# Sums of squares taken inside the embedding stage, two norm stages joined into their neighbours, and block 2's first layer opened on halves of the tokens

## The reference, cut to what matters

```python
for i in range(DEPTH):                      # block 1, DEPTH = 2
    h = rms_norm(x, g_mix[i])
    ... mixer, experts ...
    ple_gate = sigmoid(rms_norm(x, g_ple[i]) @ w_ple_gate[i])
    x = x + ple_gate * (p[i] @ w_ple[i])    # embedding stage
x = rms_norm(x, g_final)
...
for l in range(DEPTH):                      # block 2
    u = rms_norm_2(x, norm_g[l]) * (1 + scale) + shift
    z = u @ w_in[l]
    ... x = x + gate * (merged @ w_out[l])
```

## Time and profile before

| | us |
|---|---|
| median of three runs | 3681.98 (3681.97 to 3682.17) |
| profiled execution, its own time | 3682.63 |
| span of its profile | 3680.9 |
| VectorE's last addition in layer 0's embedding stage, start | 1143.27 |
| layer 1's first product, start | 1164.03 |
| the same addition in layer 1's embedding stage, start | 2278.16 |
| block 2's first product, start | 2310.16 |

### The profile page before, as it was taken

One profiled execution on the slowest core, in us unless ns is written; L12 is line 12 of the kernel. 1 busy time (PEld: TensorE's weight loads), 2 busy tenths in 40 slices (PEclk: granted clock), 3 DMA queues, 4 the chain that ended last, 5 costly groups with the idle time before them and its releaser, 6 DMA issues. The chain is left out here.

```text
span 3680.9 us, 41926 instructions
## 1 busy us (share of the span) xinstructions
PE 3421.2 (93%) x16364; PEld 2281.5 (62%) x16364; DVE 1760.2 (48%) x3023; ACT 1064.4 (29%) x1684; POOL 38.6 (1%) x42
## 2 busy tenths in 40 slices
PE   7999996999988999996999997999999999999999
PEld 5866673444446866675444445777766687777666
DVE  7766633212135875744121224467654355666443
ACT  4343322101023334322011013343333234433322
POOL 1000000000000200000000000000000000000000
PEclk9999998999998999997999998999999999999999
DMA  5521127999963441124999982212321331222213
GB/s 191 193 94 58 58 86 310 423 423 424 424 250 129 157 144 58 58 94 189 420 424 424 423 351 71 93 61 66 92 81 69 106 115 58 68 76 86 69 69 115
DMA packets 129376, 653.28 MB, mean 177 GB/s; under 512 B 22036, under 2 KB 32276, under 8 KB 62136
## 3 DMA queue, kind: packets, MB, share of 16 engines
q1 hardware_dynamic: 129208, 650.98, 45.6%
HBM read 632.54 MB, written 14.72 MB: 176 GB/s over the span
## 5 line engine op out<-in xcount | busy, mean ns | idle before, releaser
L1733 PE MATMUL ps<-normed_T_hi,ring_split 128*128 128x512 f32 x1920 | 609.8, 399 | 7.5 <-PEq L264 7.5
L1733 PEld LDWEIGHTS ps<-normed_T_hi,ring_split 128*128 128x128 f32 x1920 | 354.5, 188 | 107.4 <-issue 34.3
L1733 PE MATMUL ps<-normed_T_lo,ring_split 128*128 128x512 f32 (+1 forms) x960 | 376.1, 392 | 0.0
L2486 PE MATMUL ps<-normed_T_hi,ring_split 128*128 128x512 f32 x1024 | 336.1, 410 | 8.9 <-DVE branches L2752 7.6
L2065 DVE TENSOR_TENSOR ring_split<-weight_ring,ring_split 128x2048 fp32r<-128x2048 f32 x76 | 174.0, 2289 | 151.9 <-ACT ring_split L1921 151.6
L2486 PEld LDWEIGHTS ps<-normed_T_hi,ring_split 128*128 128x128 f32 x1024 | 192.9, 192 | 81.6 <-issue 32.7
L1733 PEld LDWEIGHTS ps<-normed_T_lo,ring_split 128*128 128x128 f32 (+1 forms) x960 | 180.2, 188 | 40.0
L2486 PE MATMUL ps<-normed_T_lo,ring_split 128*128 128x512 f32 x512 | 202.6, 396 | 0.0
L1789 PE MATMUL ps<-branches 128*128 128x512 f32 x384 | 173.0, 593 | 3.3 <-issue 3.0
L1230 PE MATMUL ps<-weight_ring,projected 128*64 128x512 f32 x768 | 167.9, 593 | 0.0
L1921 ACT ACTIVATE ring_split<-weight_ring 128x2048 fp32r<-128x2048 f32 x76 | 144.9, 1912 | 52.5 <-DMA weight_ring<-in_w_slabs 48.1
(11 more groups left out here) (443 smaller groups left out, 6028.3 us busy)
## 6 DMA issues: line engine op xcount, KB each, us to landing
weight_ring<-in_w_slabs SPq DMA_DIRECT2D x78, 1024.0 KB, 4.9
weight_ring<-in_w_exp_gate SPq DMA_DIRECT2D x48, 1024.0 KB, 16.9
weight_ring<-in_w_exp_down SPq DMA_DIRECT2D x48, 1024.0 KB, 12.2
weight_ring<-in_w_exp_up SPq DMA_DIRECT2D x48, 1024.0 KB, 20.5
weight_ring<-in_w_branch_gate SPq DMA_DIRECT2D x32, 1024.0 KB, 4.9
spare_weights<-in_w_exp_up SPq DMA_DIRECT2D x32, 1024.0 KB, 21.0
spare_weights<-in_w_exp_gate SPq DMA_DIRECT2D x32, 1024.0 KB, 20.3
spare_weights<-in_w_exp_down SPq DMA_DIRECT2D x32, 1024.0 KB, 15.7
```

The costliest lines, as they stand in the source:

```text
L1733: ins = e.matmul(dst, lhs(k, m), rhs(k, m), start=k == 0 and m == 0, stop=k == KD - 1 and m == 2)
L2486: ins = e.matmul(dst, lhs(k, m), rhs(k, m), start=k == 0 and m == 0, stop=k == KD - 1 and m == 2)
```

## The change

1. The embedding stage sums the squares itself. ScalarE squares a tile as soon as its second addition is done, tile 3 in two halves; in the last layer VectorE also multiplies each tile by `g_final` into `gained_X`, and ScalarE sums the squares of that too. With the two sums, block 2's norm of the normed rows needs no second pass: its row factor is 1/sqrt(mean(gained squares) + 1e-6 (mean square + 1e-6)).
2. The second round's products are put in another order: the first half of tile 0, then all side products, then tile by tile.
3. The embedding stage also loads and splits the next stage's slab 0, and in the last layer loads the rope table, the gain row and block 2's modulation.
4. Layer 1's `norm_stage` begins at the variance (`summed`), and has no split of slab 0.
5. `row_norm_stage` and the `norm_stage` ahead of block 2 are gone. Block 2's first layer opens on halves: tiles 0 and 1 are scaled and turned, step 0 runs on them, then tiles 2 and 3 are turned, then the other half steps. GpSimd writes the normed residual to `X`, tile by tile, and SP stores each tile.
6. Waits on the slabs' semaphores count through several stages (`slot_total`) instead of from zero.

```diff
+                    if summed:
+                        e.tensor_tensor(sums[:, 3, 0:1], sums[:, 3, 0:1], sums[:, 4, 0:1], ALU.add).then_inc(s["vector_step"], st.add("vector_step"))
+                        e.wait_ge(s[st.name], st.value)
+                        e.tensor_scalar(var, sums[:, 0:4, 0], 1.0 / D, EPS, ALU.mult, ALU.add).then_inc(s["var_ready"], 1)
...
+                            if last_layer:
+                                e.dma_start(rope_T[:, :, :], a["c_rope_T"]).then_inc(s["inputs_loaded"], 16)
+                                e.dma_start(gain_row, a["g_final"].partition_broadcast(P)).then_inc(s["inputs_loaded"], 16)
+                                e.dma_start(small[:, 136:152], modulation_saved[0, :, :]).then_inc(s["inputs_loaded"], 16)
+                    e.wait_ge(s["lo_ready"], 2)
+                    e.dma_start(ring_land[:, 0, :], next_slab).then_inc(slot_loaded[0], 16)
+                    if last_layer:
+                        e.wait_ge(s["inputs_loaded"], 48)
...
+                    for kh in range(2):
+                        if kh:
+                            e.wait_ge(s["lo_ready"], 1)
+                        for t in range(NT):
+                            exact_products(e, PS[:, t, :], t, kh, kh, 512).then_inc(s["product_ready"], 1)
+                    e.wait_ge(s["lo_ready"], 2)
+                    e.wait_ge(s["exp_done"], 1)
+                    exact_products(e, PS[:, 0, :], 0, 0, 0, 512)
+                    e.wait_ge(s["side_landed"], 16)
+                    for t in range(NT):
+                        e.wait_ge(s["gate_used"], t + 1)
+                        for k in range(2):
+                            ins = e.matmul(PS[:, 4 + t, :], p_T[:, k, t * P:(t + 1) * P], ple_side[:, k, :], start=k == 0, stop=k == 1)
+                        ins.then_inc(s["side_ready"], 1)
+                    e.wait_ge(s["lo_ready"], 3)
+                    for t in range(NT):
+                        if t:
+                            exact_products(e, PS[:, t, :], t, 0, 0, 512)
+                        exact_products(e, PS[:, t, :], t, 1, 1, 512).then_inc(s["product_ready"], 1)
...
+                    def squares(t, n, cols, done, vector_n):
+                        if st.value:
+                            e.wait_ge(s[st.name], st.value)
+                        e.wait_ge(tile_done, done)
+                        e.activation(square_out[:, cols], X[:, t, cols], ACT.Square, accum_out=sums[:, n, 0:1]).then_inc(s["squares_ready"], st.add("squares_ready"))
+                        if last_layer:
+                            e.wait_ge(s[st.name], st.value)
+                            e.wait_ge(gained, vector_n)
+                            e.activation(square_out[:, cols], gained_X[:, t, cols], ACT.Square, accum_out=sums[:, n, 1:2]).then_inc(s["squares_ready"], st.add("squares_ready"))
...
+                    e.wait_ge(slot_loaded[0], EXPERT_LOADS + 32)
+                    e.wait_ge(s["lo_ready"], 3)
+                    e.activation(ring_hi[:, 0, :], ring_land[:, 0, :], ACT.Copy).then_inc(s["slab_hi"], 1)
+                    sigmoid(1, 0)
+                    squares(0, 0, whole, 5, 1)
+                    sigmoid(1, 1)
+                    squares(1, 1, whole, 6, 2)
+                    squares(3, 4, low, 4, 3)
+                    sigmoid(1, 2)
+                    squares(2, 2, whole, 7, 4)
+                    sigmoid(1, 3)
+                    e.preload_act_table(ACT.Sqrt)
+                    squares(3, 3, high, 8, 5)
...
+                        add(0, t)
                     split(3, 1)
-                    add(1)
-                    e.wait_ge(s[st.name], st.value)
+                    e.wait_ge(s["slab_hi"], 1)
+                    e.tensor_tensor(ring_lo[:, 0, :], ring_land[:, 0, :], ring_hi[:, 0, :].bitcast(F32), ALU.subtract).then_inc(s["slab_lo"], 1)
+                    if last_layer:
+                        e.wait_ge(s["inputs_loaded"], 48)
+                    add(1, 0)
+                    gain(0, whole, 5)
+                    add(1, 1)
+                    gain(1, whole, 6)
+                    gain(3, low, 4)
+                    add(1, 2)
+                    gain(2, whole, 7)
+                    add(1, 3)
+                    gain(3, high, 8)
...
+                    else:
+                        for q in (1, 2):
+                            e.dma_start(ring_land[:, q, :], a["w_slabs_2"][l, q, :, :]).then_inc(slot_loaded[q], 16)
+                        for t in range(NT):
+                            e.wait_ge(s["pool_ready"], t + 1)
+                            e.dma_start(x_saved[t * P:(t + 1) * P, :], X[:, t, :]).then_inc(s["stored"], 16)
+                    e.wait_ge(s["stored"], 16 if half_turned else 64)
...
+                        e.wait_ge(s["scaled_by_vector"], 1)
+                        turn_tile(e, s, U, open_banks, 0, lambda pair: None)
+                        e.wait_ge(s["scaled_by_scalar"], 1)
+                        turn_tile(e, s, U, open_banks, 1, None)
+                        half_step(0, 0, lambda k: k + 1)
+                        e.wait_ge(s["scaled_by_vector"], 2)
+                        turn_tile(e, s, U, open_banks, 2, lambda pair: e.wait_ge(s["turned_taken_scalar"], 2 * pair - 2) if pair >= 2 else None)
+                        e.wait_ge(s["scaled_by_vector"], 3)
+                        turn_tile(e, s, U, open_banks, 3, None)
+                        half_step(1, 0, lambda k: 8)
+                        half_step(0, 1, lambda k: k + 9)
+                        half_step(1, 1, lambda k: 16)
...
+                @block.gpsimd
+                def _(e):
+                    if opening:
+                        e.wait_ge(s["rstd_ready"], 1)
+                        for t in range(NT):
+                            e.tensor_scalar(X[:, t, :], gained_X[:, t, :], open_rstd[:, t:t + 1], None, ALU.mult).then_inc(s["pool_ready"], 1)
...
+                        e.wait_ge(s["var_ready"], 1)
+                        e.activation(open_root, open_var, ACT.Sqrt).then_inc(s["root_ready"], 1)
+                        e.wait_ge(s["rstd_ready"], 1)
+                        e.activation(U[:, 1, :], gained_X[:, 1, :], ACT.Copy, scale=open_rstd[:, 5:6]).then_inc(s["scaled_by_scalar"], 1)
+                        take_turned(e, s, open_banks, 0, 2, range(KD), lambda k: 0)
+                        take_turned(e, s, open_banks, 1, 4, range(KD), lambda k: k + 1)
...
+                    if opening:
+                        inner(e.tensor_tensor(sums[:, 3, :], sums[:, 3, :], sums[:, 4, :], ALU.add))
+                        e.wait_ge(s[st_.name], st_.value)
+                        inner(e.tensor_scalar(open_var[:, 0:4], sums[:, 0:4, 0], 1.0 / D, EPS, ALU.mult, ALU.add))
+                        inner(e.tensor_scalar(open_var[:, 4:8], sums[:, 0:4, 1], 1.0 / D, None, ALU.mult))
+                        e.wait_ge(s[st_.name], st_.value)
+                        e.scalar_tensor_tensor(open_var[:, 4:8], open_var[:, 0:4], EPS, open_var[:, 4:8], ALU.mult, ALU.add).then_inc(s["var_ready"], 1)
+                        e.wait_ge(s["root_ready"], 1)
+                        e.reciprocal(open_rstd, open_root).then_inc(s["rstd_ready"], 1)
+                        e.wait_ge(s["rstd_ready"], 1)
+                        for t in (0, 2, 3):
+                            e.tensor_scalar(U[:, t, :], gained_X[:, t, :], open_rstd[:, 4 + t:5 + t], None, ALU.mult).then_inc(s["scaled_by_vector"], 1)
+                        split_taken(e, s, 0, range(KD), 0, st_)
+                        split_taken(e, s, 1, range(KD), 8, st_)
+                        e.wait_ge(s["stored"], 64)
...
-        row_norm_stage("g_final")
-        norm_stage([(modulation_cols, modulation_saved[0, :, :])], scale_col2, shift_col, save=True, slabs=lambda q: a["w_slabs_2"][0, q, :, :])
         for l in range(DEPTH):
-            layer2_stage(l, l > 0)
+            layer2_stage(l, "half turned" if l else "summed")
```

More of the change, by code:

```diff
@@ L255, in exact_products, with norm_stage @@
             return ins
-        def norm_stage(loads, scale_col, bias_col=None, experts_of=None, save=False, slabs=None, ple=None):
+        sums = small[:, 32:42].rearrange("p (t c) -> p t c", c=2)
+        def norm_stage(loads, scale_col, bias_col=None, experts_of=None, save=False, slabs=None, ple=None, summed=False):
             s = signals.stage()
@@ L307, in _ @@
                         turn_to_float32(e, s, KD, scale_col, bias_col)
-                    if slabs is not None:
+                    if slabs is not None and not summed:
                         e.wait_ge(s["slab_landed_0"], 16)
@@ L1325, in mixer_kernel @@
         half_var = small[:, 16:17]
+        open_var, open_root, open_rstd = (small[:, 8 * i:8 * i + 8] for i in range(3))
         final_gain, squares2 = T[:, 2048:3072], T[:, 3072:4096]
@@ L1873, in half_step @@
                         for k in range(KD):
[L1874 to L1875 removed]
+                            if split_at(k) > 0:
```

(1 more changed line is left out.)

264 lines of the change are left out of this document (123 added, 141 removed).

## The result

The changed kernel takes 3656.5 us (median of four, 3656.2 to 3657.3); the kernel before, run beside it, 3682.0 us. The ratio is 0.9933, 95% interval 0.9916 to 0.9950: faster by 25.5 us where 22.7 were forecast. The profiled execution has a span of 3654.4 us and a time of 3656.53 us.

A forecast was written before the change was run, and what follows sets the result against it. TensorE is busy 93% of the span; both joins are chains of small VectorE and ScalarE steps where it has no product. Savings 6.4 + 16.3 = 22.7 us off 3681.98 give 3659 us, range 3654 to 3666.

The forecast's parts named there:

- Join 1: End of layer 0's embedding stage to layer 1's first projections: sums 3.2 and split of slab 0 3.26, 6.4 us saved.
- What was called hidden: Layer 0's embedding stage and join 1: slab 0's split fits idle time, no gate stall, stored residual hidden by 2.8 us.
- Join 2: End of layer 1's embedding stage to block 2's projections: 18.0 of 44.4 us saved before contention, 16.3 us after it.
- The template of the earlier trace: Join 2's half steps read from block 2's second layer before the change: 6.4 us first half's splits, 9.85 us the rest.
- The term that was right for a wrong reason: Join 2: GpSimd's four residual passes, 1.3 us each (bounds 1.04 and 2.08), lock VectorE out and cost 1.7 us.
- The stores: Join 2: four 512 KB residual stores on SP, last landing about 2292.3, VectorE asking at about 2303: hidden by 10 us.
- The clock: Join 2: TensorE's clock 0.50 in the first turning (16 transposes, 3.2 us), full in the second (2.25 us with hand-over).
- rival 1: Join 2: GpSimd passes of 2.08 us and TensorE at 0.50 through the half steps; 3662 to 3666 us, chance 0.25.
- rival 2: Both joins: shorter idle keeps the clock up, saving up to 1.7 and 1.1 us, GpSimd hides; 3654 to 3657, chance 0.15.
- Where the half step was placed: Join 2: tiles 2 and 3 turned behind the first half step by the new order, 2.25 us, ending at 2295.4.

The follow-up runs named there:

- second profile: Both kernels run and profiled again, unedited; the changed one took 3654.8 us in median, ratio 0.9927 to the kernel before.
- turning first: Changed kernel with all four tiles turned ahead of block 2's first half step, instead of two, the half step and two; 3654.4 us, ratio 0.9922.
- the same useless products: Changed kernel with 24 TensorE products without use behind each embedding stage, to keep the clock up; 3656.9 us.
- cut in two at it: Changed kernel, all four tiles turned first, products without use cut to 14 before the border, 8 behind it, 6 behind layer 1's turning; 3647.4 us, ratio 0.9905.

## Why the prediction was right

**Join 1**, forecast 6.4 us, measured 6.55: the sums 3.22 (3.2), of which 1.94 came back when the sums were put back and 1.28 are the table load, by its row; the split of slab 0 3.26 by the rows (3.26), 3.0 when put back. The added square of the last half tile, the border and the small instructions came to 2.14 us (2.17). What was called hidden stayed hidden: in layer 0's embedding stage TensorE doesn't wait behind its first product, and from there to the end of the last addition the stage takes 54.15 us before and 54.17 after. In the second profile it is 55.64 us, without a wait, but with a clock of 0.72 instead of 0.85 in the stage's first 10.6 us.

**Join 2**, forecast 28.1 us from the last addition to step 2, measured 28.41 and 27.63. ScalarE's first piece comes 7.37 us behind the last addition (7.25 by the terms), the second turning takes 2.3 us (2.25), from ScalarE's second half on it is 9.82 us (9.85), and 9.84 in the second profile. The template of the earlier trace rows held to a few hundredths. Two sizes were off and nearly balance in the first profile: GpSimd's wait was shorter (see below), and the half step's products behind its last split took 1.14 us at the low clock instead of 0.6.

**The term that was right for a wrong reason** is GpSimd's, 1.7 us forecast, 1.0 to 1.4 us measured (7.4 and 7.7 against 6.4 us to the last split). A pass took 2.85 us, not 1.3, outside of the bounds of 1.04 and 2.08. These came from passes with two inputs over 512 columns, and a one-input pass over 1,024 was not twice as long but 2.7 times. And VectorE did not stand still until a pass was over: 3.3 us of waits for 12.3 us of passes, a good quarter. By the prediction's own working, in which the wait is the whole pass, 2.85 us would have cost some 8 us (an estimate: 5.0 at 2.08 us, and four times the difference). The two errors nearly cancelled, and that was luck. The earlier trace rows showed the second error already: the two scalings waited 2.75 - 1.01 = 1.74 us beside two passes of 1.04 and 1.36 us, the second of them
```profile
1219.58 1.36 POOL L780 TENSOR_TENSOR residual<-residual 128x512 f32<-128x512 f32 x1
```
so a wait was 0.87 us on average, less than a pass. The Trainium skill's page "SBUF — State Buffer", section "SBUF: two separate sides", has the loser blocked for a whole instruction; the passes here held VectorE for 0.8 of 2.85 us on average, so on this kernel the measurement decides. The Trainium skill's page "GPSIMD Engine Reference", section "Engine selection", has one-input passes at about line rate, from which I had estimated 0.85 us; the trace shows 2.85.

**The stores** were called hidden by 10 us. They were, by less: the last is issued until 2286.14, a store lands in 3.5 us at the median (2.6 in the earlier trace rows), and VectorE asks at 2295.18, so about 5.5 us are left. Slab 1's split starts at 2296.30, behind ScalarE's, so the stores would hold up the chain from some 4.7 us a pass, not 3.6 (an estimate from these figures: 6.7 us over four passes). VectorE's wait for them came in three experiments, when the passes were later and in the two where all else was sooner.

**The clock** was forecast low in the first turning and full in the second. The first turning took 3.29 us at a clock of 0.58, and 3.68 at 0.50 in the second profile, where the earlier trace rows had been read as 3.2; the last split ended 15.12 us behind the last addition either way. The clock was low through the first half step too and rose in the second turning: half of rival 1's condition, though that half step hangs on VectorE's splits.

**The surplus of 3 us** is no term of the prediction. The joins gave 22.5 us where 22.7 were forecast. The time of 3656.5 us fell into the band of rival 2, 3654 to 3657, but not by rival 2's terms. In the first profile layer 1's first 24 products took 7.10 us (7.26 before) and the first 16 transposes of join 2 3.29 (3.68 before), so the clock gave a few tenths, and GpSimd did not hide. In the second the 24 products did run at full clock, 5.54 us, but layer 1's stretch was no shorter for it (1113.3 us). The surplus lies in stretches whose length moves by 3 to 5 us between executions of the same code, and on average it came with the change; why stays open.

**Where the half step was placed** I costed as given. Between the two turnings it costs 3.4 to 4.1 us, since ScalarE idles for the tiles 2 and 3. The 3.4 are against the second profile, where the first turning ran at the same clock of 0.50 and the last split of the first half ended at the same distance. The bank waits that come with turning first are 1.6 us and are covered.

## What to carry to other kernels

Read a chain from the same chain elsewhere in the trace: the pattern of the earlier trace rows gave 9.85 for 9.82 us, while the one operation without a row of its own shape was off by a factor of two. Before filling an idle engine, find the border that waits for it: the same useless products lost 1 to 2 us at each join ahead of a stage border and, cut in two at it, gave 0.9 to 1.3 us at one and 0.7 at the other. Before a shorter stretch is put down to an edit, look whether the unedited kernel has it too in another profile. When work is split in halves to overlap, issue the cheap step that feeds the next half ahead of the long step of this one, and look which buffers this needs.

## What was not expected of the hardware

GpSimd multiplies 128x1024 by a column in 2.85 us, nearly four times VectorE's 0.75. Its passes hold VectorE up for part of their length only: 0.8 us for a pass of 1,024 columns and 0.3 for one of 512, and in a pass of 1,024 columns one operation bears nearly all of it, while others within the pass run undelayed. A turning of 16 transposes takes 3.7 us at a clock of 0.50 and 1.9 to 2.0 at 1.00. The same code comes in profiles with different clocks at the same place: layer 1's first 24 products took 7.1 us at 0.76 and 5.5 at 1.00.
